# A prologue rearranged: x loaded first, fused modulation products, position tables and neighbourhood bias moved into later stages

## The reference, cut to what matters

```python
mod = silu(c) @ w_ada[l] + b_ada[l]              # (1, 6144): first the vectors sh1 and sc1
sh1, sc1, g1, sh2, sc2, g2 = split(mod, 6)
h = rms_norm(x, norm1_g) * (1 + sc1) + sh1       # modulated input of the token mixer
proj = h @ w_in                                  # retention q, k, v, gate; attention; gate_a, gate_b
ro = retention(rotary(rq), rotary(rk), rv)       # 4 heads, then a group norm and silu(rg) * ro
s = q @ k.T * scale + bias_tab[t5_bucket(...)]   # dilated attention: position bias from rel_bias
merged = sigmoid(gate_a) * ret_out + sigmoid(gate_b) * att_out
x = x + g1 * (merged @ w_o)
x = x + g2 * (relu(modulate(rms_norm(x)) @ w_ff1) ** 2 @ w_ff2)
# second_block, both layers:
s_loc = q @ k_band * scale + rpb[:, dr, dc]      # neighbourhood attention, bias from na_rpb
lam = exp(sum(lq1 * lk1)) - exp(sum(lq2 * lk2)) + lam_init
```

## Time and profile before

| | before |
|---|---|
| median of 3 runs | 3256.82 us (3250.85 to 3258.18) |
| the profiled execution | 3258.83 us, span 3257.2 us |
| PE busy | 3036.1 us, 93% of the span |
| DVE busy | 1685.3 us, 52% |
| ACT busy | 1179.8 us, 36% |
| moved by DMA | 307.50 MB, 94 GB/s over the span |

### The profile page before, as it was taken

The page is one execution under the profiler, slowest core; times in us unless marked ns, Lnnn a source line. Parts: engine busy times, 40 slices in busy tenths (PEclk is TensorE's granted clock), DMA queues, the critical chain, the costliest instruction groups (busy, mean ns, idle before and its releaser), DMA issues.

```text
span 3257.2 us, 40990 instructions
## 1 busy us (share of the span) xinstructions
PE 3036.1 (93%) x16079; PEld 2553.1 (78%) x16079; DVE 1685.3 (52%) x2168; ACT 1179.8 (36%) x1683; POOL 102.5 (3%) x148
## 2 busy tenths in 40 slices
PE   5899999999998999989988889999999988989998
PEld 3777877888786888859887768888887967768886
DVE  4454454545554666564487455454555247444444
ACT  2232233223333433341255343232334236443443
POOL 1000000000000000000000000000000000000000
PEclk7899999999999999989998999999999999999999
DMA  8233233453432444324210112322222230113331
GB/s 273 91 104 119 93 113 119 144 155 107 131 104 84 125 134 145 107 66 128 94 36 1 40 56 80 91 84 86 88 87 65 84 86 1 39 52 97 103 97 65
DMA packets 260467, 307.50 MB, mean 94 GB/s; under 512 B 23467, under 2 KB 231739, under 8 KB 260316
## 3 DMA queue, kind: packets, MB, share of 16 engines
q1 hardware_dynamic: 234716, 224.43, 22.3%
q0 software_dynamic: 19456, 72.00, 7.2%
q10 hardware_dynamic: 6144, 8.91, 0.9%
HBM read 294.05 MB, written 11.27 MB: 94 GB/s over the span
## 4 chain that ended last, share of the span: by engine, by line
PE 84%; DVE 6%; DVEq 3%; ACT 2%; issue 2%; SPq 1%; DMA 1%; ACTq 0%
PE psum L545 24%; PE psum L546 24%; PE psum L547 24%; PE psum L874 3%; PE psum L623 2%; PE psum L884 2%; PE psum L672 2%; PE psum L715 1%; DVE w_lo L1597 1%; DVE n_t L1585 1%; SPq L436 1%; PE psum L771 1%; DVEq L1584 1%; PE psum L702 1%; ACT w_hi L1063 0%
## 5 line engine op out<-in xcount | busy, mean ns | idle before, releaser
L1597 DVE TENSOR_TENSOR w_lo<-raw,w_hi 128x2048 fp32r<-128x2048 f32 (+1 forms) x244 | 435.4, 1785 | 549.1 <-ACT w_hi L1063 382.1
L545 PE MATMUL psum<-hs_hi,w_hi 128*128 128x512 f32 x1632 | 654.8, 401 | 46.6 <-DVE hs_lo L1589 29.6
L546 PE MATMUL psum<-hs_hi,w_lo 128*128 128x512 f32 x1632 | 646.0, 396 | 0.0
L547 PE MATMUL psum<-hs_lo,w_hi 128*128 128x512 f32 x1632 | 645.3, 395 | 0.0
L545 PEld LDWEIGHTS psum<-hs_hi,w_hi 128*128 128x128 f32 x1632 | 313.4, 192 | 118.3 <-issue 40.1
L547 PEld LDWEIGHTS psum<-hs_lo,w_hi 128*128 128x128 f32 x1632 | 312.5, 191 | 66.9
L546 PEld LDWEIGHTS psum<-hs_hi,w_lo 128*128 128x128 f32 x1632 | 313.3, 192 | 65.5 <-issue 1.9
L545 PE MATMUL psum<-mid_hi,w_hi 128*128 128x512 f32 x768 | 299.5, 390 | 0.0
L546 PE MATMUL psum<-mid_hi,w_lo 128*128 128x512 f32 x768 | 299.4, 390 | 0.0
L547 PE MATMUL psum<-mid_lo,w_hi 128*128 128x512 f32 x768 | 299.1, 389 | 0.0
L1653 DVE SCALAR_TENSOR_TENSOR ada_acc<-ada_raw,csil,ada_acc 128x512 f32<-128x512 f32 x392 | 279.8, 749 | 32.4 <-DMA ada_raw<-in_w_ada 13.0
(11 more groups left out here) (330 smaller groups left out, 5043.7 us busy)
## 6 DMA issues: line engine op xcount, KB each, us to landing
raw<-in_w_in SPq DMA_DIRECT2D x56, 1024.0 KB, 5.1
ada_raw<-in_ada_w POOLq DMA_DIRECT2D x96, 512.0 KB, 4.3
raw<-in_w_ff SPq DMA_DIRECT2D x48, 1024.0 KB, 5.6
raw<-in_w_ff SPq DMA_DIRECT2D x96, 512.0 KB, 3.4
ada_raw<-in_w_ada POOLq DMA_DIRECT2D x32, 512.0 KB, 4.5
raw<-in_w_in SPq DMA_DIRECT2D x24, 512.0 KB, 4.7
ada<-in_w_ada SPq DMA_DIRECT2D x4, 2048.0 KB, 24.0
raw<-in_w_ret_out SPq DMA_DIRECT2D x16, 512.0 KB, 3.5
```

The costliest lines, as they stand in the source:

```text
L545: pe.matmul(dst, lhi, rhi, start=start, stop=False)
L546: pe.matmul(dst, llo, rhi, start=False, stop=False)
L547: return pe.matmul(dst, lhi, rlo, start=False, stop=stop)
L1597: dve.tensor_tensor(w_lo[par][:, 0:kt], raw[par][:, 0:kt], w_hi[par][:, 0:kt].bitcast(F32), ALU.subtract).then_inc(lo_done, 1)
```

## The change

- **Order of the loads.** SP issues `x_tok` and `ident` first, then the vector rows, then the four pieces of `w_ada` in the order 0, 3, 1, 2, then the weights of units 0 and 1, and only then the small ones (`lrow`, `vrow2`, `onehot`, `rel`). `ada0[3]` moves to a place of its own, so that `lo(0)` can be made before the modulation is known.
- **Fused products.** For each of `ada0[0..2]` DVE runs one multiplication and seven multiply-and-add instructions of 512 columns, with `csil` as a scalar per row, where it ran one product of 4096 columns and three sums.
- **Position tables.** `u_tab` is made in the four units of `gate_a`, one head in each, into `X0`, `X1` and `C0`; ACT copies it out and stores it by its own DMA queue. The copy `rel_b` is gone: PE reads `rel` with a step of zero.
- **`lam`, `vec2` and the clearing of `accr`** move behind head 0 (`lam_and_sums`); `vrow2` is transposed inside head 0.
- **Neighbourhood bias.** POOL clears `rpb`, loads and stores it in the first layer's feed-forward, between the loads of slots 57 to 65. SP waits for it ahead of `na_bias`.

```diff
 # SP
+            sp.dma_start(x_tok[:], d["x"].rearrange("b (t p) n -> p (b t) n", p=P)).then_inc(x_in, 16)
+            sp.dma_start(ident[:], d["ident"]).then_inc(const_in, 16)
...
-            for a in range(4):
+            for a in (0, 3, 1, 2):
                 sp.dma_start(ada0[a][:], wada[:, :, a * 512:(a + 1) * 512]).then_inc(ada0_in[a], 16)
+            load(0, 0, cols(win, RQ0))
+            load(1, 1, cols(win, RK0))
...
-            for head in range(ATT_HEADS):
-
-                sp.wait_ge(u_read, 3 * head + 3)
-                sp.dma_start(u_dram[head], u_tab[head % 2][:]).then_inc(u_out[head % 2], 16)
 # PE, head 0
+                if first:
+                    pe.wait_ge(vrow2_in, 16 * 2 * len(V2))
+                    pe.transpose(C1[:, P:2 * P], vrow2[:], ident[:]).then_inc(v2_t, 1)
 # PE, gate_a
+            def bias_table(head):
+
+                if head == 0:
+                    pe.wait_ge(rel_in, 32)
+                    pe.wait_ge(o_evac, 16)
+                    pe.wait_ge(gstd_done, 4)
+                else:
+                    pe.wait_ge(u_read, 3 * head)
...
+                for c, dst in enumerate((X0, X1)):
+                    pe.matmul(dst[:], rel_b(head), onehot[:, 512 * c:512 * c + 512], start=True, stop=True).then_inc(u_done, 1)
+                pe.matmul(C0[:, 0:256], rel_b(4 + head), onehot[:, 1024:1280], start=True, stop=True)
+                pe.matmul(C0[:, 256:512], rel_b(8 + head), onehot[:, 1280:1536], start=True, stop=True).then_inc(u_done, 1)
+
             for j in range(4):
                 gemm(FU["gate_a"] + j, j % 2, hs_hi, hs_lo)
+                bias_table(j)
                 ada_turns("gate_a", j)
 # ACT
             ret_head(0, 0, False, lambda j: hi(j))
+            act.wait_ge(lam_dot, 1)
+            act.activation(lam[:, 0:4], lam[:, 0:4], ACT.Exp).then_inc(lam_exp, 1)
             with act.Fori(0, RET_HEADS - 1) as i:
...
+                if j >= 2:
+                    act.wait_ge(u_out[j % 2], 16)
+                for c, src in enumerate((X0, X1, C0)):
+                    act.wait_ge(u_done, 3 * j + c + 1)
+                    act.copy(u_tab[j % 2][:, 512 * c:512 * c + 512], src[:]).then_inc(u_read, 1)
+                act.wait_ge(u_read, 3 * j + 3)
+                act.dma_start(u_dram[j], u_tab[j % 2][:]).then_inc(u_out[j % 2], 16)
 # DVE
             for a in range(3):

                 w_ = ada0[a]
+                if a == 2:
+                    norm_rstd()
                 dve.wait_ge(ada0_in[a], 16)
-                dve.tensor_tensor(w_[:], w_[:], bass.AP(csil, 0, [csil[:].ap[0], [1, KT], [0, 512]]), ALU.mult)
-                for k in (4, 2, 1):
+                dve.tensor_scalar(w_[:, 0], w_[:, 0], csil[:, 0:1], None, ALU.mult)
+                for k in range(1, KT):
                     dve.drain()
-                    last = dve.tensor_tensor(w_[:, 0:k], w_[:, 0:k], w_[:, k:2 * k], ALU.add)
+                    last = dve.scalar_tensor_tensor(out=w_[:, 0], in0=w_[:, k], scalar=csil[:, k:k + 1], in1=w_[:, 0],
+                                                    op0=ALU.mult, op1=ALU.add)
                 last.then_inc(ada0_sum, 1)
-                if a == 1:
-                    norm_rstd()
+            lo(0, 0)
             dve.wait_ge(ada0_done, 1)
...
             ret_head(0, 0, False)
+            lam_and_sums()
             with dve.Fori(1, RET_HEADS) as h:
 # POOL
+            for s in range(56, 80):
+                pool.wait_ge(ada_sum, s - 1)
+                load_ada(wada2[0], 512 * ((s - 32) // 4), s % 4, s % 2)
+                if s == 57:
+                    pool.wait_ge(hs_ready, 16)
+                    for buffer in rpb:
+                        pool.memset(buffer[:], 0.0)
+                    pool.drain()
+                    nb_load(0)
+                elif 58 <= s < 66:
+                    i = s - 58
+                    if i < 7:
+                        nb_load(i + 1)
+                    nb_store(i)
```

More of the change, by code:

```diff
@@ L527, in _ @@
                 sp.wait_ge(rot_read, 4 * l + 4)
+                if l == 0:
+                    for stored in nb_out:
+                        sp.wait_ge(stored, 64)
                 for h in range(4):
@@ L627, in _ @@
             norm_sums()
-            pe.wait_ge(rel_ready, 2)
-            for head in range(ATT_HEADS):
-                for c in range(3):
-                    i = 3 * head + c
-                    if i >= 2:
-                        pe.wait_ge(u_read, i - 1)
-                    g = 0 if c < 2 else 1
-                    dst = G[2 + i % 2]
-                    if c < 2:
-                        mm = pe.matmul(dst[:], rel_b[:, head, :], onehot[:, 512 * c:512 * c + 512], start=True, stop=True)
-                    else:
-                        pe.matmul(dst[:, 0:256], rel_b[:, 4 + head, :], onehot[:, 1024:1280], start=True, stop=True)
-                        mm = pe.matmul(dst[:, 256:512], rel_b[:, 8 + head, :], onehot[:, 1280:1536], start=True, stop=True)
-                    mm.then_inc(u_done, 1)
-            pe.wait_ge(vrow2_in, 16 * 2 * len(V2))
-            pe.wait_ge(v3_done, 1)
-            pe.transpose(X1[:, 0:P], vrow2[:], ident[:]).then_inc(v2_t, 1)
             pe.wait_ge(csil_ready, 1)
@@ L660, in _ @@
             mm.then_inc(ada0_done, 1)
-            pe.wait_ge(u_read, 12)
             pe.wait_ge(xt_read, 8)
@@ L1130, in _ @@
             norm_hi(mod1[:, 0:KT], 0)
-            for stored in u_out:
-                act.wait_ge(stored, 32)
-            act.wait_ge(lam_dot, 1)
-            act.activation(lam[:, 0:4], lam[:, 0:4], ACT.Exp).then_inc(lam_exp, 1)
             def ret_head(h, n, with_out, next_hi):
@@ L1236, in _ @@
                     act.wait_ge(zlo_done, 4)
+                    for stored in u_out:
+                        act.wait_ge(stored, 32)
                     for r_ in range(4):
@@ L1561, in _ @@
             dve.memset(stat[:], 0.0).then_inc(y_free, 3)
-            for buffer in rpb:
-                dve.memset(buffer[:], 0.0).then_inc(rpb_zero, 1)
-            dve.drain()
-            dve.wait_ge(rel_in, 32)
-            dve.tensor_copy(rel_b[:], bass.AP(rel, 0, [rel[:].ap[0], [1, 12], [0, P]])).then_inc(rel_ready, 1)
             dve.wait_ge(csil_ready, 1)
@@ L1617, in _, with lam_and_sums @@
             dve.drain()
[L1618 removed]
             norm_apply(X, scale1[:, 0, :], mod1[:, 0:8], 0)
[L1621 to L1635 removed]
+            def lam_and_sums():
+                dve.wait_ge(lam_in, 64)
+                dve.tensor_tensor(ldot[:], lrow[:, 0:4:2], lrow[:, 1:4:2], ALU.mult)
+                dve.drain()
+                dve.tensor_reduce(lam[:, 0:4], ldot[:].rearrange("p a b c -> p (a b) c"), AX.X, ALU.add).then_inc(lam_dot, 1)
+                dve.wait_ge(v3_done, 2)
+                dve.wait_ge(lam_exp, 1)
+                for l in range(2):
+                    dve.tensor_scalar(lam[:, l:l + 1], lam[:, l:l + 1], lam[:, 2 + l:3 + l], LAM_INIT[l], ALU.subtract, ALU.add)
+                dve.drain()
+                dve.tensor_scalar(lam[:, 0:2], lam[:, 0:2], -1.0, None, ALU.mult)
+                dve.memset(accr[:], 0.0)
             def ada_slot(s, i=None, two=True):
@@ L2240, in _, with nb_load, nb_store @@
             loads(wada, 2560, 4, 7)
-            for l in range(2):
-                loads(wada2[l], 0, 32 + 48 * l, 12)
+            loads(wada2[0], 0, 32, 6)
+            def nb_load(i):
+                if i >= 2:
+                    pool.wait_ge(nb_out[i % 2], 16 * (i // 2))
+                src = bass.AP(d["na_rpb_2"].tensor, i * NB_DR * (2 * NA_COLS - 1),
+                              [[0, GRID], [2 * NA_COLS - 1, NB_DR], [1, 2 * NA_COLS - 1]])
+                pool.dma_start(rpb[i % 2][:, :, GRID - NA_COLS:GRID + NA_COLS - 1], src).then_inc(rpb_in[i % 2], 16)
+            def nb_store(i):
+                pool.wait_ge(rpb_in[i % 2], 16 * (i // 2 + 1))
+                pool.dma_start(nb_dram[i // 4, i % 4], rpb[i % 2][:].rearrange("p r w -> p (r w)")).then_inc(nb_out[i % 2], 16)
+            for s in range(56, 80):
[12 more added lines that the diff above has]
+                    nb_store(i)
+            loads(wada2[1], 0, 80, 12)
 def constants():
```

66 lines of the change are left out of this document (14 added, 52 removed).

## The result

The changed kernel takes 3235.77 us (median of 4 runs, 3229.60 to 3237.53) against 3257.50 for the kernel before on the same chip (4 runs, 3250.85 to 3258.59). The ratio is 0.9931, its 95% interval 0.9916 to 0.9947: faster by 22 us, which is clear of the noise but only 0.7%, where 37 us were predicted; the median lies 0.8 us above the predicted range. Its profiled execution took 3235.11, span 3233.4.

The account below looks back on a forecast made before the run. It took the prologue as bound by an order of work, and PE as the bound behind it. Terms -42.0 - 7.7 + 5.9 + 2.6 + 4.6 = -36.6 gave 3222.2 us for the profiled execution, 3220 for the median, range 3209 to 3235.

Parts of the forecast that it names:

- 3 x 2.57 - 3.1 = +4.6: `gate_a`: three tables cost 2.57 us each, the first is free, and keeping the clock up gives 3.1 back.
- the zero for every stage far from the edits: Stages the edits do not touch: no term in the sum, so 0 us.
- Prologue, -42.0: Start to unit 0: pieces of `w_ada` land earlier, unit 0 begins at about 48.5 instead of 90.50, -42.0 us.
- The other worry: Prologue: PE's `w_ada` products all at the lower clock put unit 0 at 52.5; kept as +4 in the range.
- Unit 1, -7.7: Unit 1 begins about 13.8 us after unit 0 instead of 19.8; -7.7 us in all, bounds -4 and -8.2.
- rival 4: First units wait for weights, as rope, decay and units 2 and 3 are issued late: 3250 us, chance 0.03.
- the -2.1: Part of unit 1's -7.7 not written out; elsewhere the prediction says matmuls lost 2 us in unit 1.
- a gap below 1 us: Sign of being right: unit 1 less than 1 us behind unit 0 and at full clock.
- `lam`, +5.9: Behind head 0: the `lam` chain and clearing of `accr` delay what PE waits for, +5.9 us, bounds 5.2 and 7.3.
- the table load, +2.6: Loop over heads: ACT's cast gets a 1.28 us table load, on the path in heads 2 and 3, +2.6 us.
- Rival 1: Moved work costs its full price: products at lower clock, tables 10.3, `lam` 7.3; 3231 us, chance 0.2.
- Neighbourhood bias, 0: First layer's feed-forward: POOL's bias loads, stores and clearing are covered between slots, 0 us.

Follow-up runs that it names:

- e0_again: The changed kernel run once more with nothing edited: median 3233.64 us, ratio 0.9913 to the kernel before.
- e8_full: Changed kernel with `rope` wait moved, `lam` chain inside head 0, three position tables in heads 1 to 3, table matmuls over 128 rows: 3187.28 us.
- e1_rope: Changed kernel with VectorE's wait for `rope` moved from ahead of unit 1's low part to ahead of the rotation: 3228.74 us.
- e2_lam: Changed kernel with the `lam` chain, its Exp and the clearing of the head sums moved into head 0: 3213.34 us.
- e4_pad: Changed kernel with the position tables' matmuls over 128 rows instead of 33, the rest zeros: 3225.18 us.
- e3_onecol: Changed kernel with the sixteen position-table matmuls writing one column each, all waits, copies and stores kept: 3228.87 us.

## Why the prediction came out too low

Two steps of the prediction failed above all. One is the price of the tables in `gate_a`, "3 x 2.57 - 3.1 = +4.6", which measured +9.3: the first table did not keep the clock up, and each of the others costs more than 2.57. The other is the zero for every stage far from the edits, put there without a reason: the layer-0 stage measured +7.3 in the profiled execution. The miss of the range itself is close to chance: e0_again, the same kernel, has a median of 3233.64, which lies inside it. The terms decide.

*Prologue, -42.0: right in mechanism, 2.6 short.* The arrival of `ada0[1]` was put "at 27": it landed at 29.65. By 28 us 9.6 million bytes had come (291 GB/s to 12 us, 375 to 20, 387 to 28), which would do for x, both slots and three pieces (9.4), but a part of them belonged to the fourth piece and to what stood behind it. The rate was right: the first piece is used at 18.91 and the third to be loaded at 29.65, so two pieces (4.2 million bytes) take 10.7 us, 391 GB/s. The delay lies ahead of the first piece, which at the prediction's rate would have come at about 16. The fused piece (6.2) and the reciprocal (3.35) took what was written; from `mod` to the first matmul it took 3.4 and not 2.9. The other worry, TensorE at the lower clock, came true (11.62 us, near the 13.44) without setting the time: in e8_full the products took 9.11, TensorE waited 2.41 us for VectorE, and unit 0 began at the same time within 0.2 us. By the undoings, the fused form is worth 4.9 us of the 39.4, the order of loads 6.6, the neighbourhood bias 2.7; the rest was the tables and the products behind them, which I didn't undo.

*Unit 1, -7.7: missed a wait.* "`lo(1)` now follows the modulated input" left out that the wait for `rope` stands in front of it in VectorE's program; that SP issues `rope` only when the modulated input is done stands in rival 4, but was drawn on only for the weights. e1_rope gives 13.65 us, where 13.8 were predicted. The clock did stay up, behind a wait of 1.75 us, and the -2.1 were right; but that a gap below 1 us leaves the clock up is no rule that the runs bear out, as it fell in `gate_a` behind 0.31.

*`lam`, +5.9, and the table load, +2.6: right in mechanism* (4.6 and 2.9), and e2_lam gives both back. The 4.6 lie below the lower bound of 5.2: the chain of `lam` took 5.9 us (146.00 to 151.85) instead of 7.3, mainly as VectorE waited 0.34 us for the Exp where it had waited 1.63. Before and after:

```profile
103.10 0.34 DVE L1627 TENSOR_SCALAR lam<-lam 128x1 f32<-128x1 f32 x2 [1.63 <-ACT lam L1135]
```

```profile
147.00 0.34 DVE L1623 TENSOR_SCALAR lam<-lam 128x1 f32<-128x1 f32 x2 [0.34 <-ACT lam L1169]
```

The Trainium skill, page ScalarE: Activation LUTs, section What ACT_TABLE_LOAD costs, counts about 2.66 us for a switch with its drain; taking one load out of a pass gave 1.41 here, near the row's 1.28, and the measurement decides.

*Tables in `gate_a`, +4.6: mis-sized, the largest miss of my own.* That the first one is free held. But each of the three others costs 3.0 us and not 2.57, with 0.32 in front of a table and a slower first matmul behind it; and the -3.1 "if it keeps the clock up" did not come, as the clock fell although TensorE hardly waited. e4_pad shows what made it fall: not the 0.31 us of waiting, nor the one-column products alone, but the 33-row matmuls ahead of them. Rival 1 had named the full price of 10.3 for this term.

*Neighbourhood bias, 0: right.* VectorE nowhere waits for `ada_raw` in the first feed-forward.

*Far from the edits: +7.3.* "A stage far from the edits that has become longer" was on the list of what would make the prediction wrong, but had no term in the sum, and it was so in the profiled execution. Without it the sum is -31.1, which gives 3227.7 for the profiled execution; e1_rope, e3_onecol and e4_pad, near to the changed kernel and profiled without it, have medians of 3225 to 3229. So of the 12.8 us between forecast and profile 7.3 are a stage of two lengths, which I had not looked for in a profile of one execution; 4.7 are `gate_a`, 2.6 the prologue, 1.6 `rope`, and -3.4 small ones the other way (1.3 of them `lam`, 1.9 in the attention, which no run explains).

## What to carry to other kernels

Before you price a moved instruction, read the whole program order of the engine that gets it: one of the misses here is a wait (`rope`) that stands in front of something else, and the switch of tables at the top of the loop could be priced only because that order was read. Work taken out of a bound stage goes where the trace shows the bound engine waiting, not where it fits by name: three tables that cost 3.0 us each between units cost next to nothing in a wait of 3.29. And look in more than one profile of the kernel before whether its stages have one length.
